# The preparation of a scan's decay rows, re-ordered on three engines: turns one tile later, ScalarE's second part behind two roundings, VectorE's copies spread over the convolutions

## The reference, cut to what matters

```python
dt = softplus(dt_raw + dt_bias)
a = -exp(a_log)
a_cum = cumsum(dt * a)            # over chunks
decay = exp(a_cum[:, :, -1:] - a_cum)
chunk_decay = exp(a_cum[:, :, -1])
states = einsum('bcsgn,bcsgr,bcsgrp->bcgrpn', bm, decay, xdt)
y_off = einsum('bclgn,bcgrpn,bclgr->bclgrp', cm, prev, exp(a_cum))
```

## Time and profile before

| | |
|---|---|
| median of 3 runs | 1778.78 us (1777.37 to 1779.04) |
| the profiled execution | 1779.58 us |
| its span | 1777.9 us |
| TensorE busy | 1731.1 us, 97% |
| VectorE / ScalarE / GpSimd busy | 713.5 / 589.9 / 687.4 us |
| mean granted TensorE clock | 0.992 |

### The profile page before, as it was taken

The page is one execution under the profiler, slowest core; times in us unless marked ns, Lnnn a source line. Parts: engine busy times, 40 slices in busy tenths (PEclk is TensorE's granted clock), DMA queues, the critical chain, the costliest instruction groups (busy, mean ns, idle before and its releaser), DMA issues.

```text
span 1777.9 us, 21509 instructions
## 1 busy us (share of the span) xinstructions
PE 1731.1 (97%) x7890; PEld 1409.5 (79%) x7890; DVE 713.5 (40%) x1224; ACT 589.9 (33%) x801; POOL 687.4 (39%) x295
## 2 busy tenths in 40 slices
PE   7999999999999999999899999999989999999997
PEld 6888888888888888888788888887848787878886
DVE  4222322223111324111642644627499544454227
ACT  5333322333222224112642323323262343352120
POOL 3433343333444444443244433333314333324451
PEclk9999999999999999999899999999999999999999
DMA  5423222322333333433144242333303222227332
GB/s 198 127 91 89 91 89 89 101 89 83 99 96 94 95 95 116 145 118 95 69 171 153 84 126 88 119 107 107 94 24 96 80 74 83 71 71 244 124 106 95
DMA packets 55499, 186.12 MB, mean 105 GB/s; under 512 B 5848, under 2 KB 6104, under 8 KB 54272
## 3 DMA queue, kind: packets, MB, share of 16 engines
q1 hardware_dynamic: 46080, 160.52, 29.1%
q10 hardware_dynamic: 9344, 24.55, 3.9%
HBM read 176.57 MB, written 8.47 MB: 104 GB/s over the span
## 4 chain that ended last, share of the span: by engine, by line
PE 89%; DVE 8%; issue 1%; ACT 1%; POOL 0%; DMA 0%; SPq 0%; DVEq 0%; ACTq 0%; POOLq 0%
PE bank L367 87%; PE bank L371 2%; DVE bias L1132 2%; DVE bias L1600 1%; DVE top L1596 1%; POOL w_lo L347 0%; ACT w_hi L748 0%; DVE padded L1384 0%; DVE feats L1132 0%; DMA raw<-in_stream 0%; DVE rope_q L1475 0%; DVE padded L1383 0%; DVE planes_lo L1327 0%; ACT L1048 0%; DVE kT L1386 0%
## 5 line engine op out<-in xcount | busy, mean ns | idle before, releaser
L347 POOL TENSOR_TENSOR w_lo<-raw,w_hi 128x1024 fp32r<-128x1024 f32 x276 | 669.9, 2429 | 1050.9 <-ACT w_hi L748 1050.8
L367 PE MATMUL bank<-planes_hi,w_hi 128*128 128x512 f32 (+1 forms) x1792 | 709.1, 396 | 20.1 <-DVE w_lo L1194 9.6
L367 PE MATMUL bank<-planes_lo,w_hi 128*128 128x512 f32 (+1 forms) x1792 | 694.7, 388 | 0.0
L367 PE MATMUL bank<-planes_hi,w_lo 128*128 128x512 f32 (+1 forms) x1776 | 687.9, 387 | 0.0
L748 ACT ACTIVATE w_hi<-raw 128x1024 fp32r<-128x1024 f32 x278 | 294.7, 1060 | 1048.1 <-PE bank L367 1018.5
L367 PEld LDWEIGHTS bank<-planes_hi,w_hi 128*128 128x128 f32 x1792 | 339.9, 190 | 94.4 <-issue 21.5
L367 PEld LDWEIGHTS bank<-planes_lo,w_hi 128*128 128x128 f32 x1792 | 339.8, 190 | 70.7 <-issue 4.8
L367 PEld LDWEIGHTS bank<-planes_hi,w_lo 128*128 128x128 f32 x1776 | 336.2, 189 | 68.3
L367 PE MATMUL bank<-w_hi,planes_hi 128*128 128x512 f32 x496 | 194.2, 391 | 0.0
L367 PE MATMUL bank<-w_hi,planes_lo 128*128 128x512 f32 x496 | 193.0, 389 | 0.0
L367 PE MATMUL bank<-w_lo,planes_hi 128*128 128x512 f32 x496 | 193.0, 389 | 0.0
(11 more groups left out here) (260 smaller groups left out, 1201.5 us busy)
## 6 DMA issues: line engine op xcount, KB each, us to landing
raw<-in_stream SPq DMA_DIRECT2D x282, 512.0 KB, 3.6
h_rows<-feats ACTq DMA_DIRECT2D x4, 1024.0 KB, 7.0
out<-feats ACTq DMA_DIRECT2D x7, 512.0 KB, 2.7
feats<-in_x_t SPq DMA_DIRECT2D x3, 1024.0 KB, 10.7
rope_q<-cum_dram ACTq DMA_DIRECT2D x8, 256.0 KB, 3.1
bias<-in_x_rows ACTq DMA_DIRECT2D x2, 1024.0 KB, 6.2
probs<-in_x_rows ACTq DMA_DIRECT2D x2, 1024.0 KB, 8.0
rope_q<-decay_dram SPq DMA_DIRECT2D x8, 256.0 KB, 5.5
```

The costliest lines, as they stand in the source:

```text
L347: nc.gpsimd.tensor_sub(w_lo[:, s, :], raw[:, s, :], w_hi[:, s, :].bitcast(fp32)).then_inc(lo_ready, 1)
L367: return nc.tensor.matmul(o, a, b, start=start, stop=stop)
```

## The change

On TensorE `prepare()` moves from behind tile 1 to behind tile 2, and `spread_decay()` from behind tile 2 to behind tile 3. On ScalarE the second part becomes `prepare_exps()` and is called in the loop, behind the second rounding of k = 0. On VectorE the product L1418 becomes `prepare_scaled()`, behind `conv_tile(0)`, and `take_prepared()` moves behind `conv_tile(1)`. No instruction is added or removed.

```diff
@@ TensorE
                 ssd_tile(6 * it + 1)
-                if g < 0:
-                    prepare()
-                else:
+                if g >= 0:
                     ssd_states(g)
                 ssd_tile(6 * it + 2)
                 if g < 0:
+                    prepare()
+                ssd_tile(6 * it + 3)
+                if g < 0:
                     spread_decay()
-                ssd_tile(6 * it + 3)
-                if g >= 0:
+                else:
                     ssd_head(g, 0)
@@ ScalarE
-            act.wait_ge(prep_turn, 3)
-            step(nc.scalar.activation(R[1], R[1], ACT.Exp))
-            signal(nc.scalar.activation(R[2], cumT[:, :], ACT.Exp), prep_turn, 4)
-            act.dma_start(decay_dram[0:SSD_HEADS, :], cumT[:, :]).then_inc(decay_kept, 16)
-            act.dma_start(decay_dram[SSD_HEADS:2 * SSD_HEADS, :], R[2]).then_inc(decay_kept, 16)
+
+            def prepare_exps():
+
+                act.wait_ge(prep_turn, 3)
+                step(nc.scalar.activation(R[1], R[1], ACT.Exp))
+                signal(nc.scalar.activation(R[2], cumT[:, :], ACT.Exp), prep_turn, 4)
+                act.dma_start(decay_dram[0:SSD_HEADS, :], cumT[:, :]).then_inc(decay_kept, 16)
+                act.dma_start(decay_dram[SSD_HEADS:2 * SSD_HEADS, :], R[2]).then_inc(decay_kept, 16)
...
                 round_unit(m + 1, 2 * p + 1)
+                if n == 0:
+                    prepare_exps()
@@ VectorE
-            dve.wait_ge(prep_turn, 4)
-            signal(V.tensor_mul(R[1], R[1], R[0]), prep_turn, 5)
+
+            def prepare_scaled():
+
+                dve.wait_ge(prep_turn, 4)
+                signal(V.tensor_mul(R[1], R[1], R[0]), prep_turn, 5)
...
             conv_tile(0)
+            prepare_scaled()
+            conv_tile(1)
             take_prepared()
-            conv_tile(1)
             conv_tile(2)
             take_decay()
             conv_tile(3)
```

## The result

The changed kernel takes 1780.97 us (median of 20 runs, 1779.74 to 1781.88), the kernel before 1778.38 (20 runs, 1777.12 to 1779.40). The ratio is 1.0015 with an interval of 1.0009 to 1.0021: 2.6 us slower, 1.6 to 3.7, most of it inside the 0.2% that I called no change. The profiled execution took 1780.38 us for a span of 1778.7.

A forecast was written before the change was run, and what follows sets the result against it. TensorE was taken as the bound, with 89% of the chain that ended last. Tile 2 0.13 us later plus 1.41 us of turns made +1.5 us, so 1780.3 us against 1778.78; range 1776.3 to 1782.4 us.

The forecast's parts named there:

- The port: GpSimd's two early subtractions hold two of VectorE's four scans at the shared SBUF port; its chain ends 4.1 us late.
- The first two rivals: VectorE's chain: port does not hold, -4.3 us, chance 0.10; or only the L1412 are held, -0.3 to -2.0 us, chance 0.13.
- The order that was saved: VectorE's conv 0 starts right behind the chain, not behind L1418: 3.4 us saved, spent at the port.
- The turns: TensorE's 20 small transposes of prepare, moved between tiles 2 and 3, cost their full price there: 1.41 us.
- The rival of the falling clock: Small turns amid full work lower TensorE's clock, tile 3 starts at 1.2 GHz: +3.2 to +3.9 us, chance 0.07.
- The clock in the hole: TensorE's empty time before tile 2 stays as long, so tile 2's 1.7 us of slow matmuls stay.
- what moves TensorE here moves the end, unless a later wait swallows it: TensorE holds 89% of the chain that ended last, so its shift at the edited stretch reaches the end.
- The copies, ScalarE's and VectorE's queues: Later take_prepared, conv 2 and tile 3's roundings and low parts are hidden by margins of 6 to 10 us: cost 0.

The follow-up runs named there:

- round_late: The changed kernel, but ScalarE waits for the end of VectorE's chain before tile 2's two roundings; 1775.3 us, ratio 0.9981 to the kernel before.
- pool_waits: The changed kernel, early roundings kept, but GpSimd waits for the end of VectorE's chain before tile 2's two subtractions; 1774.74 us, ratio 0.9981 to the kernel before.
- one_rounding: The changed kernel with one of tile 2's two roundings moved behind ScalarE's Exps, so one subtraction falls on VectorE's chain; 1777.93 us, ratio 0.9999 to the kernel before.
- turns_alone: The kernel before with only TensorE's turns, spread_decay and VectorE's take_prepared moved as in the change; 1781.35 us, ratio 1.0018.
- extra_40: The kernel before with 40 more small turns behind tile 3, into a bank nobody reads then; 1783.17 us, ratio 1.0028.
- extra_20: The kernel before with a second copy of the 20 turns behind tile 3, into a bank nobody reads then; 1780.83 us, ratio 1.0015.
- after_again: The changed kernel as it is, timed once more against the kernel before; 1781.62 us, ratio 1.0017.
- turns_back: The changed kernel with TensorE's turns back between tiles 1 and 2 and spread_decay between 2 and 3; 1781.2 us, ratio 1.0017 to the kernel before.

## Why the prediction was right, and where its sum was short

**The port.** This was the step on which the sign hung, and it held. Forecast: two of four scans at 2.5 us, the chain 4.1 us late, tile 2 0.13 us later than before. Found: 2.53 and 2.43 us, 4.1 us, 0.13 us. Shown by round_late, pool_waits and one_rounding, which take away both subtractions or one without changing any instruction that computes. The rule of the Trainium skill that I set beside it (SBUF — State Buffer, "Who interferes with whom") agrees with all of them. The first two rivals, that the port does not hold the scans, fell with the scans' 5.88 us. What the first one promised if the port were free, -4.3 us, is about what pool_waits gives (-4.0 in the profile, -3.3 timed).

**The order that was saved.** Conv 0 no longer waits for L1418, and starts 3.5 us less behind the chain; the chain ends 4.1 us later. The gain was real and was given back at the port, and 0.6 us more. Tile 2 still started only 0.13 us later, since before it waited for GpSimd, 0.5 us beyond conv 0.

**The turns.** Forecast 1.41 us; turns_alone shows 1.45 as a whole, and the chain of pool_waits has 1.34 for the piece. The clock stayed at 1.00 behind them. The rival of the falling clock was wrong for this kernel and right in kind: extra_40 shows it with twice as many turns. The Trainium skill's sentence on transposes (TensorE: Matmul & The Clock Gate, "PE-mode transpose") gives no size: extra_40, where the clock fell, agrees with it, and the 20 turns here and in extra_20 cost no clock. Whether the transposing or the 16 columns brought it down no run shows.

**The clock in the hole.** I left its 1.7 us as they were: 12.68 us for tile 2 by the chain, about 0.1 more than before. As a difference that was right. As a size 1.7 was a little too much: in round_late, pool_waits and one_rounding, where the hole is 1.9 to 4.0 us shorter, tile 2 takes 11.13 to 11.19 us at 1.00 of the clock, so the slow matmuls cost about 1.5 us.

**What was missing.** The step of my text that fell short is "what moves TensorE here moves the end, unless a later wait swallows it". It lets a later wait take from a shift and never add to it, and the sum has no term behind tile 3. The restart behind the key search took 0.9 us more, so the sum was short of the 2.6 us measured by 1.1. In the kernel before, the first of its matmuls still run at 2.4 GHz and the clock falls after them; in the changed one it is down from the start and comes back later. Two windows of each, before and then changed:

```profile
1393.00:1395.00 2.00, 0.76 (x4) 0.69 (x5) 1.42 (x2) 1.56 (x3) 0.64 (x1) 0.93 0.06 16
...
1398.00:1399.00 1.00, 1.00 (x5) 0.67 (x4) 0.60 (x1) 0.67 (x2) 0.00 (x0) 0.93 0.00 0
```

```profile
1393.00:1395.00 2.00, 0.86 (x3) 0.87 (x4) 1.11 (x2) 1.49 (x2) 0.53 (x1) 0.50 0.28 45
...
1398.00:1399.00 1.00, 1.00 (x3) 0.39 (x3) 0.44 (x2) 0.71 (x2) 0.00 (x0) 0.50 0.00 0
```

extra_20 has it without the change. In nine of ten profiles the restart took either 15.0 or 15.9 to 16.1 us. Kernels with about the same shift agree (the four at +1.45 to +1.69 have 15.94 to 16.11, the two at -3.5 and -4.0 have 15.0), but the cost does not rise or fall with the shift: -1.88 has 16.08 and +3.33 has 15.03. What decides stays open.

A rival has to be named, since each other kernel has one profile only: such a restart also differs between two executions of one kernel. The 48 matmuls in front of the edit, in the changed kernel and then in after_again, which is the same kernel:

```profile
863.13 7.48 PE bank L367 x48
```

```profile
864.42 7.96 PE bank L367 x48
```

Against it as the whole explanation: those two profiles agree on the late restart (15.95 and 16.01), and turns_alone's timed runs are 1.6 to 4.8 us above the kernel before, which 1.45 us alone would not give. So the extra microsecond is in the timed runs too, but that the shift is its cause is the best reading of the profiles and not shown beyond them. With 0.9 us added, my sum is 2.4 us against 2.6 measured.

**The copies, ScalarE's and VectorE's queues.** Nothing behind the move was late: in this stretch TensorE's only new wait is tile 2's for conv 0.

## What to carry to other kernels

Work moved earlier on one engine starts its followers earlier too. Ask which instructions those will now run beside: here ScalarE's roundings were free, and GpSimd's subtractions behind them held two scans of VectorE for 2 us each. When a hole is longer than you want, look for what can be made to wait harmlessly; a single wait that holds GpSimd back for 3 us turned +3 into -3 us. And small work that lies in a hole is free only there: before moving it out, see whether the hole closes.

## What the runs showed of the hardware that I had not expected

- A restart of TensorE 480 us behind the edit takes 15.0 us in four profiles and 15.9 to 16.3 us in six, for the same 56 matmuls. Small shifts in front of it go with the one or the other; what decides is not shown.
- Behind forty turns of 16 columns (2.7 us) between full tiles the granted clock fell to 0.50, and they cost 4.45 us up to group 0, in place of the 2.7 expected. Twenty (1.4 us) left it at 1.00.
- The same sixteen turns take 1.86 us at a granted clock of 0.50 (turns_back) and 1.14 us at 1.00, though each has only 16 columns.
